# Spreading the gate grids of a PEER layer over 60 blocks, accumulating gathered rows beside them, and holding two gathered rows in flight in the value stage

## The chip, the core and the metric

The kernel runs on one core of a Trainium2 chip. The metric is the device time of one execution in microseconds, the median of several runs; lower is better. In the profile PE is TensorE, PEld its weight loads, DVE is VectorE, ACT is ScalarE, POOL is GpSimd and SP is SyncE; a trailing q marks the queue of an engine that issues DMAs.

## The reference, cut to what matters

One layer of a conditioned hybrid decoder runs on 512 prompt tokens and 64 sample tokens (576 in all). Its first half (norm, input projection, three kinds of mixers, output projection) is not touched. Its second half is PEER: 16384 single-neuron experts, of which each token chooses 16 in each of 8 heads.

```python
q = (xb @ w_q).reshape(PEER_BLOCK, PEER_HEADS, 2, PEER_DQ // 2)
scores = jnp.einsum('bhsd,hskd->bhsk', q, sub_keys).astype(jnp.float32)
sv, si = lax.top_k(scores, PEER_TOPK)
...
top_v, top_pos = lax.top_k(cand, PEER_TOPK)
eidx = jnp.take_along_axis(cidx, top_pos, axis=-1)
gate = jax.nn.softmax(top_v, axis=-1)
u_sel = jnp.take(u_tab, eidx, axis=0)
act = jax.nn.gelu(jnp.einsum('bhkd,bd->bhk', u_sel, xb))
v_sel = jnp.take(v_tab, eidx, axis=0)
return jnp.einsum('bhk,bhkd->bd', gate * act, v_sel)
```

Here `u_tab` and `v_tab` hold 16384 rows of 2048 floats each. So each token's output is a sum of 128 rows of the value table, each weighted by its gate times its activation.

## The kernel before

The tokens are in two groups. For 320 of them, the dense tokens, the kernel multiplies the whole value table with a coefficient matrix (expert by token, zero where an expert was not chosen). For the other 256, the row tokens, it gathers the chosen value rows with indirect DMAs, 128 tokens at a time: gather `s` fetches for each of 128 tokens one row of 2048 floats, and there are 256 gathers (`NSP`), 128 for each half of the row tokens. All matrix products of this half are made of three products each (high times high, low times high, high times low part), so each weight block needs its high part, rounded by ACT (`high`), and its low part, a subtraction on DVE (`low`).

The second half of the program runs in these stages:

- Query blocks, then **row blocks**: 128 blocks of the table `peer_ut`, each times the 256 row tokens. Their activations go to a table in memory. Beside them DVE finds the top 16.
- **Gate stage**: the next 30 blocks of `peer_ut` (a second pass over the table), each times the 320 dense tokens. Beside them the gate grids are made: for each group of 4 dense tokens (80 groups) DVE makes one-hot matrices (L1713 to L1715, three operations, called a hot set here), PE multiplies them (`gate_products`, L2273: four 128x128 products, each of them two instructions in the trace, "x8"), ACT copies the grid out of PSUM into one of two staging tiles (L1065), and after 8 groups ACT sends a staging tile to `gate_scratch`. The loop runs `GL` = 5 times over 6 blocks and 16 grids; PE makes a grid after every sixth of the 96 chunks of such a turn (a block has 16 chunks, a chunk is three products, L2210 to L2212). The double-buffered one-hot tiles lie in the region that begins at `C0`, and so do both staging tiles.
- **Plain stage**: the remaining 98 blocks of `peer_ut`, which end at block `NB_ALL` = 272. Since the staging tiles lie where gathered rows go (`v_rows`, four places), gathers can start only once the last staging tile is saved. DVE adds 120 gathers (`NSP_EARLY`) here, one or two behind a `low`, from the eighth block on (`rows_block`), by a multiply and add of 128x2048 floats each (L1735, `add_rows`).
- **Value stage**: 256 steps (`UNITS`), each a half row block of `peer_v`: ACT rounds it (L1090), DVE subtracts (L1749), PE does 8 chunks of three products (L2299 to L2301). Coefficient factors come back from memory every 8 steps (`load_factors`), are multiplied (L1755), rounded and split (L1759). Every 8 steps DVE adds eight PSUM banks to an accumulator (L1770, `add_half`). The other 136 gathers are added here, at five of every eight steps at most (`rows_step`).

Every engine works through its instructions in program order, and semaphores order the engines. A block or half block lies in a ring (three blocks, six halves): SP loads the next when PE is done with the one before it in the ring. On POOL, `act_column` fetches one column of activations for the row tokens (128 single numbers) and `value_rows` one gather. Before, POOL fetches the first 128 columns during the gate stage, then waits for the saved staging tiles, then issues a column and a gather alternately. Gather `s` waits until DVE has used gather `s-4`, so up to four are under way or waiting in their places.

```python
def value_rows(s):
    if s >= ROWS:
        pool.wait_ge(rows_used, s - ROWS + 1)
```

Of the kernel before, what the change touches and what calls it, by code (L numbers as in the profile page):

```python
# [7 lines left out]
ALU = mybir.AluOpType  # L8
# [7 lines left out]
P = 128  # L16
# [21 lines left out]
NSP, NSP_EARLY = 256, 120  # L38
# [37 lines left out]
def build(nc, a, o):  # L76

    ctx = ExitStack()
    with ctx:
# [179 lines left out]
        stage = [at(C0 + s * NK * TBLK, NK * TBLK).rearrange("p (i t) -> p i t", t=TBLK) for s in range(2)]  # L259
        o_j = [at(C0 + 8192 + s * 512, 512).rearrange("p (t n) -> p t n", n=P) for s in range(2)]  # L260
        o_i = [at(C0 + 9216 + s * 512, 512).rearrange("p (t n) -> p t n", n=P) for s in range(2)]
# [18 lines left out]
        v_rows = [at(C0 + D * k, D) for k in range(ROWS)]  # L280
# [116 lines left out]
        GB = NB_ROWS + 6 * GL  # L397
# [15 lines left out]

        def rows_block(s):
            return GB + 8 + s * (NB_ALL - GB - 8) // NSP_EARLY

# [43 lines left out]
        def _(sp):  # L460
# [108 lines left out]
            for k in range(2):  # L569
                sp.wait_ge(g_saved[k], 16 * (GL + 1))  # L570
            load_value(0)
# [24 lines left out]
        def _(pool):  # L596
# [119 lines left out]
            def act_column(k, s):  # L716
                pool.indirect_dma_start(out=acts[k][:, s:s + 1], out_offset=None, in_=act_table,  # L717
                                        in_offset=bass.IndirectOffsetOnAxis(ap=act_ids[k][:, s:s + 1], axis=0)
                                        ).then_inc(act_in[k], 16)

            def value_rows(s):
                if s >= ROWS:
                    pool.wait_ge(rows_used, s - ROWS + 1)
                pool.indirect_dma_start(out=v_rows[s % ROWS], out_offset=None, in_=v_table,  # L724
                                        in_offset=bass.IndirectOffsetOnAxis(ap=row_ids[s // P][:, s % P:s % P + 1], axis=0)
                                        ).then_inc(rows_in[s % ROWS], 16)
# [4 lines left out]
            for s in range(P):  # L731
                act_column(0, s)
            for k in range(2):
                pool.wait_ge(g_saved[k], 16 * (GL + 1))
            for s in range(NSP):
                if s < P:
                    act_column(1, s)
                value_rows(s)

        @block.scalar  # L740
        def _(act):
# [317 lines left out]
            with act.Fori(0, GL) as w:  # L1059
                for u in range(16):  # L1060
                    k = u // 8
                    if u % 8 == 0:
                        act.wait_ge(g_saved[k], w * 16 + 16)
                    act.wait_ge(g_made, w * 16 + u + 3)
                    act.activation(stage[k][:, :, 4 * (u % 8):4 * (u % 8) + 4].rearrange("p i t -> p t i"),  # L1065
                                   bank(6 + u % 2).rearrange("p (t i) -> p t i", i=P), ACT.Copy).then_inc(g_out, 1)
                    if u % 8 == 7:
                        act.wait_ge(g_out, w * 16 + u + 3)
                        act.dma_start(gd[:, bass.ds(w * 2 + k, 1)].rearrange("p b i t -> p (b i) t"),
                                      stage[k]).then_inc(g_saved[k], 16)  # L1070
                    if u in (1, 4, 7, 9, 12, 15):
                        n = NB_ROWS + (1, 4, 7, 9, 12, 15).index(u)
                        gelu_out(w * 6 + n, n % 3, w * 32 + uses(n), TD)
                        high(None, (n + 2) % 3, w * 32 + 16 * ((n + 2) // 3 + 1))
                        save(w * 6 + n, n % 3, dense_place(w * 6 + n), TD)
# [48 lines left out]
        def _(dve):  # L1124
# [582 lines left out]
            with dve.Fori(0, GL) as w:  # L1707
                step.enter(w, 32)
                for u in range(16):
                    n = w * 16 + u  # L1710
                    dve.wait_ge(g_made, n + 1)
                    idx = [p_selT[:, r, bass.ds(n * 4, 4)].unsqueeze(2).broadcast_to(t4_) for r in range(3)]
                    step(tt(o_e, io, idx[0], ALU.is_equal))  # L1713
                    step(tt(o_i[u % 2], o_e, idx[2], ALU.mult))
                    tt(o_j[u % 2], io, idx[1], ALU.is_equal).then_inc(oh_made, 1)  # L1715
                    if u in (0, 2, 5, 8, 10, 13):
# [683 lines left out]
```

## Time and profile before

| | before |
|---|---|
| median of 3 runs | 4622.29 us (4620.33 to 4625.47) |
| the profiled execution | 4624.3 us, of which the span from first to last instruction is 4622.6 us |
| PE busy | 4352.7 us, 94% of the span |
| DVE busy | 2851.7 us, 62% |
| ACT busy | 1273.7 us, 28% |
| POOL busy | 997.4 us, 22% |
| DMA | 993.88 MB, 215 GB/s in the mean |
| mean granted TensorE clock | 0.957 of full speed |

The shares are means over stages with very different limits. The page also cuts the span into 40 equal slices of about 116 us: there the DMA digit is 4 to 5 in the gate stage and 9 from the plain stage to almost the end, and the clock digit is 8 and 9. What is to be read is the stage from 2572 us, where the dense tokens' blocks begin, to 4576 us, where the value stage's products end.

### The profile page before, as it was taken

To read this page: it belongs to the slowest core of one execution; us is meant where nothing else is said; L and a number is where in the kernel's file an instruction comes from. 1 tells how busy PE (TensorE), PEld (TensorE's weight loads), DVE (VectorE), ACT (ScalarE), POOL (GpSimd) and SP (SyncE) were. 2 spreads that over 40 slices of the span, in tenths; PEclk is the share of its full clock that TensorE was granted. 3 is DMA by queue.
4 is the path that set the end of the run, shared out by engine and by line. 5 is a ranking of instruction groups with operands and counts; after the bars stand their busy time and mean duration, and the time that the engine had idled before them with its cause. 6 is when DMAs were issued, how large, how long until landed. Compare 5 with 4: busy or idle time off the path is not lost.

```text
span 4622.6 us, 71225 instructions
## 1 busy us (share of the span) xinstructions
PE 4352.7 (94%) x29748; PEld 4011.5 (87%) x29748; DVE 2851.7 (62%) x3848; ACT 1273.7 (28%) x1431; POOL 997.4 (22%) x619
## 2 busy tenths in 40 slices
PE   5799999999989699999999888999999999999997
PEld 3577778776679699999999888899999999999997
DVE  0479321323453423888887555477777789888896
ACT  1000101211122212433444344333333333333332
POOL 1000000001100000000000570166666434333440
PEclk8899999998779899999999999999999999999999
DMA  7311212126752222666666444599999999999994
GB/s 302 94 72 41 77 47 79 37 73 233 270 215 99 76 76 84 205 204 204 205 204 205 162 149 149 205 359 368 369 366 374 335 353 362 356 358 350 360 367 157
DMA packets 239177, 993.88 MB, mean 215 GB/s; under 512 B 42920, under 2 KB 117096, under 8 KB 158488
## 3 DMA queue, kind: packets, MB, share of 16 engines
q1 hardware_dynamic: 152376, 652.83, 40.1%
q0 software_dynamic: 48320, 279.88, 15.7%
q10 hardware_dynamic: 38304, 58.74, 3.3%
q8 instruction: 120, 1.97, 0.2%
q14 instruction: 57, 0.47, 0.0%
HBM read 917.71 MB, written 73.64 MB: 214 GB/s over the span
## 4 chain that ended last, share of the span: by engine, by line
PE 83%; DMA 8%; DVE 4%; issue 2%; ACT 2%; DVEq 0%; SPq 0%; ACTq 0%
PE PS L2210 12%; PE PS L2211 12%; PE PS L2212 12%; PE PS L2080 12%; PE PS L2299 5%; PE PS L2300 5%; PE PS L2301 5%; PE PS L2083 5%; DMA arena<-in_peer_v 4%; DMA arena<-in_w_ada 2%; PE PS L1852 2%; PE PS L2189 1%; PE PS L2191 1%; PE PS L2190 1%; PE PS L2273 1%
## 5 line engine op out<-in xcount | busy, mean ns | idle before, releaser
L2210 PE MATMUL PS<-h_hi,blk_hi 128*128 128x256 f32 (+1 forms) x4608 | 1386.4, 301 | 41.0 <-DVE h_lo L1600 32.8
L2211 PE MATMUL PS<-h_lo,blk_hi 128*128 128x256 f32 (+1 forms) x4608 | 1374.8, 298 | 0.0
L2212 PE MATMUL PS<-h_hi,blk_lo 128*128 128x256 f32 (+1 forms) x4608 | 1374.1, 298 | 0.0
L2210 PEld LDWEIGHTS PS<-h_hi,blk_hi 128*128 128x128 f32 x4608 | 885.5, 192 | 44.4 <-issue 22.6
L1606 DVE TENSOR_TENSOR blk_lo<-arena,blk_hi 128x2048 fp32r<-128x2048 f32 x272 | 623.5, 2292 | 454.3 <-ACT blk_hi L998 408.4
L2211 PEld LDWEIGHTS PS<-h_lo,blk_hi 128*128 128x128 f32 x4608 | 885.7, 192 | 0.0
L2212 PEld LDWEIGHTS PS<-h_hi,blk_lo 128*128 128x128 f32 x4608 | 884.4, 192 | 0.0
L724 POOL DMA_INDIRECT arena<-in_peer_v,attw x256 | 561.3, 2193 | 728.2 <-DVE arena L1735 653.9
L2299 PE MATMUL PS<-co_hi,ev_hi 128*128 128x320 f32 x2048 | 636.7, 311 | 23.3 <-DVE ev_lo L1749 17.8
L2300 PE MATMUL PS<-co_lo,ev_hi 128*128 128x320 f32 x2048 | 634.8, 310 | 0.0
L2301 PE MATMUL PS<-co_hi,ev_lo 128*128 128x320 f32 x2048 | 634.5, 310 | 0.0
L2080 PE MATMUL PS<-arena 128*128 128x288 f32 x2176 | 551.4, 414 | 2.2 <-ACT arena L799 2.2
L998 ACT ACTIVATE blk_hi<-arena 128x2048 fp32r<-128x2048 f32 x272 | 518.8, 1907 | 64.0 <-DMA arena<-in_peer_ut 61.4
L2080 PEld LDWEIGHTS PS<-arena 128*128 128x128 f32 x2176 | 417.4, 194 | 120.8 <-issue 2.6
L1090 ACT ACTIVATE ev_hi<-arena 128x1024 fp32r<-128x1024 f32 x256 | 271.7, 1062 | 582.2 <-DMA arena<-in_peer_v 400.3
L2299 PEld LDWEIGHTS PS<-co_hi,ev_hi 128*128 128x128 f32 x2048 | 385.9, 188 | 27.4 <-DVE ev_lo L1749 21.7
L2300 PEld LDWEIGHTS PS<-co_lo,ev_hi 128*128 128x128 f32 x2048 | 386.0, 188 | 0.0
L2301 PEld LDWEIGHTS PS<-co_hi,ev_lo 128*128 128x128 f32 x2048 | 385.9, 188 | 0.0
L717 POOL DMA_INDIRECT attw<-row_activation_scratch,cap x128 | 160.1, 1251 | 1020.2 <-DMA row_activation_scratch<-arena 978.5
L1749 DVE TENSOR_TENSOR ev_lo<-arena,ev_hi 128x1024 fp32r<-128x1024 f32 x256 | 311.4, 1218 | 87.7 <-ACT ev_hi L1090 85.3
L1009 ACT ACTIVATE arena<-PS 128x256 f32<-128x256 f32 (+1 forms) x256 | 105.1, 410 | 871.7 <-PE PS L2212 854.6
L1735 DVE SCALAR_TENSOR_TENSOR arena<-arena,attw 128x2048 f32<-128x2048 f32 x127 | 298.0, 2346 | 3.5 <-DVE arena L1735 0.5
(437 smaller groups left out, 4720.8 us busy)
## 6 DMA issues: line engine op xcount, KB each, us to landing
arena<-in_peer_ut SPq DMA_DIRECT2D x256, 1024.0 KB
arena<-in_peer_v SPq DMA_DIRECT2D x256, 512.0 KB, 8.0
arena<-in_w_ada SPq DMA_DIRECT2D x48, 2048.0 KB, 9.2
arena<-in_w_f SPq DMA_DIRECT2D x17, 2048.0 KB, 8.1
activation_scratch<-arena ACTq DMA_DIRECT2D x128, 160.0 KB
gate_scratch<-arena ACTq DMA_DIRECT2D x10, 2048.0 KB
arena<-activation_scratch SPq DMA_DIRECT2D x32, 640.0 KB, 11.8
arena<-gate_scratch SPq DMA_DIRECT2D x32, 640.0 KB, 14.5
```

The source lines that it names most:

```text
L724: pool.indirect_dma_start(out=v_rows[s % ROWS], out_offset=None, in_=v_table, in_offset=bass.IndirectOffsetOnAxis(ap=row_ids[s // P][:, s ...
L998: act.activation(blk_hi[k][:, :], blk_raw[k], ACT.Copy).then_inc(blk_hi_made, 1)
L1606: tt(blk_lo[k][:, :], blk_raw[k], blk_hi[k][:, :].bitcast(F32), ALU.subtract).then_inc(blk_lo_made, 1)
L1735: ins = stt(acc_rows[k], row, col, acc_rows[k], ALU.mult, ALU.add)
L1749: tt(ev_lo[k % RAWS][:, :], ev_raw[k % RAWS], ev_hi[k % HIS][:, :].bitcast(F32), ALU.subtract).then_inc(ev_lo_made, 1)
L2080: ins = mm(bank(job % 2, 0, HALF), w[:, c, P * (j // 2):P * (j // 2) + P], hT[:, c, HALF * (j % 2):HALF * (j % 2) + HALF], start=c == 0, s ...
L2210: mm(out, hi[:, c], h_part[0][:, c, cols], start=c == 0, stop=False)
L2211: mm(out, hi[:, c], h_part[1][:, c, cols], start=False, stop=False)
L2212: ins = mm(out, lo[:, c], h_part[0][:, c, cols], start=False, stop=c == KC - 1)
L2299: mm(out, ev_hi[k % HIS][:, w], co_hi[n % COS][:, :], start=i == 0, stop=False)
L2300: mm(out, ev_hi[k % HIS][:, w], co_lo[n % COS][:, :], start=False, stop=False)
L2301: ins = mm(out, ev_lo[k % RAWS][:, w], co_hi[n % COS][:, :], start=False, stop=i == RND - 1)
```

## The change

The gate stage now takes 60 blocks (`GBLK` = 12 for each of the 5 turns, still 16 grids a turn), and the plain stage 68. The first staging tile moves out of the gathered rows' region, into the part of the low-part tile of the activations that only the row blocks used, as 16 pieces of 256 columns; the second staging tile and the one-hot tiles are packed into the first three row places. The gathers get a fifth place (`ROWS + 1`), and in the gate stage they use two places, the fourth and the fifth (`row_place`). In the gate stage DVE adds one gather behind each `low` from the fifth block on, 56 in all (`NSP_GATES`); in the plain stage it adds 92 (up to `NSP_EARLY` = 148), with four places as before; 108 are left for the value stage, and from gather 148 on each waits until gather `s-2` is used, so that two are under way. DVE makes each hot set two or more groups ahead of PE. The activation columns come 16 ahead of the gathers (`ACOL`) and are multiplied by their gates in pieces of 16. SP's first value load waits until the 56 gathers are used, since the fifth place lies on its buffer.

```diff
-NSP, NSP_EARLY = 256, 120
+NSP, NSP_GATES, NSP_EARLY = 256, 56, 148
+ACOL, GBLK = 16, 12
...
-        stage = [at(C0 + s * NK * TBLK, NK * TBLK).rearrange("p (i t) -> p i t", t=TBLK) for s in range(2)]
...
+        stage = [at(0, KC * T).rearrange("p (c t) -> p c t", t=T)[:, :, TD:T], at(C0, NK * TBLK)]
...
-        v_rows = [at(C0 + D * k, D) for k in range(ROWS)]
+        v_rows = [at(C0 + D * k, D) for k in range(ROWS + 1)]
...
-        GB = NB_ROWS + 6 * GL
+        GB = NB_ROWS + GBLK * GL
...
+        def row_place(s):
+
+            return (ROWS - 1, ROWS)[s % 2] if s < NSP_GATES else s % ROWS
...
         def rows_block(s):
-            return GB + 8 + s * (NB_ALL - GB - 8) // NSP_EARLY
+            return GB + 3 + (s - NSP_GATES) * (NB_ALL - GB - 4) // (NSP_EARLY - NSP_GATES)
...
+            sp.wait_ge(rows_used, NSP_GATES)
             load_value(0)
...
             def value_rows(s):
-                if s >= ROWS:
-                    pool.wait_ge(rows_used, s - ROWS + 1)
...
+                if row_clear(s):
+                    pool.wait_ge(rows_used, row_clear(s) if s < NSP_EARLY else s - 1)
...
-            for s in range(P):
-                act_column(0, s)
-            for k in range(2):
-                pool.wait_ge(g_saved[k], 16 * (GL + 1))
+            for c in range(ACOL):
+                act_column(c)
+            pool.wait_ge(sel_made, 3)
             for s in range(NSP):
-                if s < P:
-                    act_column(1, s)
+                if s + ACOL < NSP:
+                    act_column(s + ACOL)
+                if s == NSP_GATES:
+                    for k in range(2):
+                        pool.wait_ge(g_saved[k], 16 * (GL + 1))
                 value_rows(s)
...
-                    if u in (1, 4, 7, 9, 12, 15):
...
+                    if u % 4 < 3:
+                        n = NB_ROWS + u // 4 * 3 + u % 4
...
+            one_hots(0)
+            one_hots(1)
+            for b in range(GBLK * GL):
+                low(NB_ROWS + 1 + b, (NB_ROWS + 1 + b) % 3)
+                if b >= GBLK * GL - NSP_GATES:
+                    add_rows(placed)
+                    placed += 1
+                for u in ((2,), (3, 4), (5,))[b % 3]:
+                    if b // 3 * 4 + u < 16 * GL:
+                        one_hots(b // 3 * 4 + u)
...
-                    if at_ % 6 != 5:
+                    if at_ % GBLK != GBLK - 1:
```

DVE at the start of the gate stage, before: the end of the first hot set of a turn, a block's `low` (L1606), and the next hot set (L1713 to L1715). ISA and REGISTER_ALU rows are waits and their arithmetic.

```order
L1715 TENSOR_TENSOR arena<-iota,arena 128x512
L1605 ISA
L1606 TENSOR_TENSOR blk_lo1_60<-arena,blk_hi1_63 128x2048
L1711 REGISTER_ALU
L1713 ISA
L1713 TENSOR_TENSOR arena<-iota,arena 128x512
L66 REGISTER_ALU
L1714 ISA
L1714 TENSOR_TENSOR arena<-arena 128x512
```

DVE in the gate stage, after, from the sixth block's `low` (L1628) on: a gather is added (L1744), then one or two hot sets (L1752 to L1754).

```order
L1628 TENSOR_TENSOR blk_lo0_59<-arena,blk_hi0_62 128x2048
L1744 SCALAR_TENSOR_TENSOR arena<-arena,attw 128x16x128
L1752 TENSOR_TENSOR arena<-iota,arena 128x512
L1753 TENSOR_TENSOR arena<-arena 128x512
L1754 TENSOR_TENSOR arena<-iota,arena 128x512
L1628 TENSOR_TENSOR blk_lo1_60<-arena,blk_hi1_63 128x2048
L1744 SCALAR_TENSOR_TENSOR arena<-arena,attw 128x16x128
L1752 TENSOR_TENSOR arena<-iota,arena 128x512
```

Before, hot sets 0 and 1 of a turn stand on either side of the first `low`; now both are made ahead of the loop, and a gather stands between each `low` and the hot sets behind it.

POOL from the gate stage on, before: 128 columns (L717), then a wait for the saved staging tiles, then columns and gathers (L724).

```order
L717 DMA attw<-row_activation_scratch,cap 128x1 [waits pool_step,a1_saved,a2_saved,a0_saved,idx_made]
L717 DMA attw<-row_activation_scratch,cap 128x1 x127
L717 DMA gla_mask<-row_activation_scratch,siluc 128x1 [waits stage1_saved,stage0_saved]
L724 DMA arena<-in_peer_v,attw 128x2048
L717 DMA gla_mask<-row_activation_scratch,siluc 128x1
```

POOL from the gate stage on, after: the columns are L735 and the gathers L742.

```order
L735 DMA attw<-row_activation_scratch,cap 128x1 [waits pool_step,a1_saved,a2_saved,a0_saved,idx_made]
L735 DMA attw<-row_activation_scratch,cap 128x1 x15
L735 DMA attw<-row_activation_scratch,cap 128x1 [waits sel_made]
L742 DMA arena<-in_peer_v,attw 128x2048
L735 DMA attw<-row_activation_scratch,cap 128x1
```

The first gather moved from behind 129 columns and the staging tiles to behind 17 columns; the wait for the staging tiles now stands in front of gather 56.

## Rows read from the trace of the kernel before

**Rows 1.** Stretches: us, PE, PEld, DVE, ACT, POOL busy; clock; DMA share; GB/s.
```profile
2572.00:2953.00 381.00, 315.39 (x2099) 307.50 (x2098) 227.26 (x269) 153.42 (x141) 160.10 (x128) 0.93 0.42 146
2953.00:3644.00 691.00, 690.09 (x4692) 687.87 (x4691) 496.32 (x219) 224.44 (x196) 439.57 (x249) 1.00 0.96 362
3644.00:4576.00 932.00, 908.66 (x6144) 904.52 (x6144) 807.16 (x811) 319.15 (x384) 337.05 (x135) 0.99 0.92 342
```

**Rows 2.** Timeline of PE, gate stage: start, duration, line, [idle before, releaser].
```profile
2683.05 1.05 PE L2273 MATMUL PS<-arena 128*128 128x128 f32 x8
2686.58 1.05 PE L2273 MATMUL PS<-arena 128*128 128x128 f32 x8
```

**Rows 3.** Timeline of PE, gate stage, around one wait.
```profile
2652.54 0.31 PE L2212 MATMUL PS<-h_hi,blk_lo 128*128 128x320 f32 x1
2655.33 1.86 PE L2273 MATMUL PS<-arena 128*128 128x128 f32 x8 [2.48 <-issue]
```

**Rows 4.** Timeline of ACT and of DVE, gate stage, before the same wait.
```profile
2648.44 0.44 ACT L1009 ACTIVATE arena<-PS 128x320 f32<-128x320 f32 x1 [0.61 <-ACT arena L1065]
2648.78 1.91 ACT L998 ACTIVATE blk_hi<-arena 128x2048 fp32r<-128x2048 f32 x1
...
2650.72 2.29 DVE L1606 TENSOR_TENSOR blk_lo<-arena,blk_hi 128x2048 fp32r<-128x2048 f32 x1 [4.16 <-issue]
2652.92 0.69 DVE L1713 TENSOR_TENSOR arena<-iota,arena 128x512 f32<-128x512 f32 x1
...
2655.20 0.68 DVE L1713 TENSOR_TENSOR arena<-iota,arena 128x512 f32<-128x512 f32 x1
```

**Rows 5.** Who waited for whom in 2572 to 2953: us in total, times, longest.
```profile
PEld PS L2273 <- DVE arena L1715: 43.8, 18, 2.9
...
PEld PS L2273 <- issue: 29.7, 12, 2.9
```

**Rows 6.** Plain stage: one stretch as in rows 1, and DVE's timeline.
```profile
3022.00:3072.00 50.00, 50.00 (x342) 49.80 (x341) 35.54 (x16) 16.52 (x15) 29.45 (x18) 1.00 0.97 379
...
3026.47 4.80 DVE L1735 SCALAR_TENSOR_TENSOR arena<-arena,attw 128x2048 f32<-128x2048 f32 x2
```

**Rows 7.** DMA issues by line: out<-in, count, KB each, median us to landing.
```profile
arena<-in_peer_ut SPq DMA_DIRECT2D x256, 1024.0 KB
...
activation_scratch<-arena ACTq DMA_DIRECT2D x128, 160.0 KB
```

**Rows 8.** POOL's columns: duration ns min/median/max, first and last start.
```profile
L717 POOL DMA_INDIRECT attw<-row_activation_scratch,cap x128: 940/1130/2916, 2579.7 to 2780.3; - x128
```

**Rows 9.** Who waited for whom in 3644 to 4576: us in total, times, longest.
```profile
ACT ev_hi L1090 <- DMA arena<-in_peer_v: 400.3, 151, 15.3
...
PEld PS L2299 <- DVE ev_lo L1749: 21.7, 15, 5.0
```

**Rows 10.** Timeline of DVE, value stage, five gathers in eight steps.
```profile
4200.26 3.57 DVE L1770 TENSOR_TENSOR arena<-arena,PS 128x320 f32<-128x320 f32 x8 [0.99 <-PE PS L2301]
...
4221.89 1.22 DVE L1749 TENSOR_TENSOR ev_lo<-arena,ev_hi 128x1024 fp32r<-128x1024 f32 x1
4223.02 0.48 DVE L1759 TENSOR_TENSOR co_lo<-arena,co_hi 128x320 fp32r<-128x320 f32 x1
4223.43 2.34 DVE L1735 SCALAR_TENSOR_TENSOR arena<-arena,gla_mask 128x2048 f32<-128x2048 f32 x1
4225.69 1.22 DVE L1749 TENSOR_TENSOR ev_lo<-arena,ev_hi 128x1024 fp32r<-128x1024 f32 x1
...
4228.76 3.26 DVE L1770 TENSOR_TENSOR arena<-arena,PS 128x320 f32<-128x320 f32 x8
```

**Rows 11.** Timeline of POOL and DVE, value stage: one gather and its use.
```profile
4414.50 2.41 POOL L724 DMA_INDIRECT arena<-in_peer_v,attw  x1 [11.00 <-issue]
4419.81 1.68 POOL L724 DMA_INDIRECT arena<-in_peer_v,attw  x1 [1.66 <-DVE arena L1735]
...
4424.71 2.35 DVE L1735 SCALAR_TENSOR_TENSOR arena<-arena,gla_mask 128x2048 f32<-128x2048 f32 x1 [0.64 <-DMA arena<-in_peer_v,attw]
```

More of the change, by code:

```diff
@@ L1706, in _ @@
             io = iota[:, :].unsqueeze(1).broadcast_to(t4_)
[L1707 to L1716, printed above, removed]
-                        b = NB_ROWS + 1 + (0, 2, 5, 8, 10, 13).index(u)
-                        low(w * 6 + b, b % 3)
-            step.leave(GL)
             def add_rows(s):
-                if s in (0, P):
-                    k = s // P
-                    dve.wait_ge(act_in[k], 16 * P)
-                    step(tt(acts[k], acts[k], gates[k], ALU.mult))
+                if s == 0:
                     dve.wait_ge(blk_made, NB_ROWS)
+                if s % ACOL == 0:
+                    g, part = s // ACOL, slice(s % P, s % P + ACOL)
+                    dve.wait_ge(act_in[g % 2], 16 * ACOL * (g // 2 + 1))
+                    step(tt(acts[s // P][:, part], acts[s // P][:, part], gates[s // P][:, part], ALU.mult))
                 k, col = s // P, acts[s // P][:, s % P:s % P + 1]
-                row = v_rows[s % ROWS].rearrange("p (c t) -> p c t", t=P)
-                dve.wait_ge(rows_in[s % ROWS], 16 * (s // ROWS + 1))
+                row = v_rows[row_place(s)].rearrange("p (c t) -> p c t", t=P)
+                dve.wait_ge(rows_in[row_sem(s)], row_fills(s))
                 if s in (0, P):
@@ L1738, in _, with one_hots @@
             placed = 0
+            def one_hots(u):
+                dve.wait_ge(g_made, u + 1)
+                idx = [p_selT[:, r, 4 * u:4 * u + 4].unsqueeze(2).broadcast_to(t4_) for r in range(3)]
+                step(tt(o_e, io, idx[0], ALU.is_equal))
+                step(tt(o_i[u % 2], o_e, idx[2], ALU.mult))
+                tt(o_j[u % 2], io, idx[1], ALU.is_equal).then_inc(oh_made, 1)
+            one_hots(0)
[8 more added lines that the diff above has]
+                        one_hots(b // 3 * 4 + u)
+            assert placed == NSP_GATES
             for n in range(GB + 1, NB_ALL):
@@ L2274, in gate_products @@
                     ins.then_inc(g_made, 1)
-                for b in range(6):
-                    block_product(w * 6 + (NB_ROWS + b), (NB_ROWS + b) % 3, (DENSE_COLS,), lambda x: gate_products(x, b))
+                for b in range(GBLK):
+                    block_product(w * GBLK + (NB_ROWS + b), (NB_ROWS + b) % 3, (DENSE_COLS,), lambda x: gate_products(x, b))
             with pe.Fori(0, (NB_ALL - GB) // 3) as i:
```

39 lines of the change are left out of this document (24 added, 15 removed).

## The prediction, made before the changed kernel ran

> **What bounds the kernel now.** I first read the three stretches that the change touches [rows 1]. The gate stage takes 381 us for 30 blocks, with PE busy 315.4 us and its clock at 0.93 in the mean. The plain stage takes 691 us for 98 blocks, PE busy 690.1 us at full clock: 7.05 us a block. The value stage takes 932 us, PE busy 908.7. So in all three PE is the bound where nothing holds it up; the question is what holds it up. In the plain stage nothing does, and DMA stands at 0.96 there with 362 GB/s, while in the gate stage it stands at 0.42 with 146 GB/s. The load on memory is uneven, and so is that on DVE.
>
> Next, PE's timeline in the gate stage. At full pace two grids start 3.53 us apart [rows 2]. Between them lie 18 products of 7.05/48 = 0.147 us, 2.64 us, so a grid costs 0.89 us. The stage's own work is 30 x 7.05 + 80 x 0.89 = 211.5 + 71.2 = 282.7 us. It takes 381, so 98.3 us are lost; 381 - 315.4 = 65.6 of them idle. The list of waits says for whom: a grid waits for DVE's last one-hot 18 times and for "issue" 12 times [rows 5]. The second is the same wait with its releaser not seen: the grid at 2655.33 [rows 3] starts just behind the hot set that ends by 2655.28. That is 30 waits in 30 blocks, one for each. The same grid lasts 1.86 us instead of 1.05 [rows 2, 3]: behind an idle time PE runs at half clock for a while, and that is the other 98.3 - 65.6 = 32.7 us, about 1.1 us a wait.
>
> Why one a block: ACT leaves the block before at 2648.44, rounds the next block's weights from 2648.78 on, DVE, idle for 4.16 us, subtracts from 2650.72 and makes the hot set only behind that, from 2652.92 on, 2.28 us a set [rows 4]. By then PE waits: its products ended at 2652.54 + 0.31 and it needs the set [rows 3]. It is the order of DVE's program, not its load, which is 227 of 381 us [rows 1].
>
> **Term 1, grids over 60 blocks.** Before, the first 60 blocks take 381 + 30 x 7.05 = 592.5 us. After, if no grid waits, they take 60 x 7.05 + 71.2 = 494.2. Gain 98.3. Three blocks and four grids are then 24.7 us. Does DVE fit? Three subtractions at a start-to-start of 2.2 and three gathers at 2.35 make 13.7, four hot sets at 2.28 make 9.1: 22.8 of 24.7 us, 92%. It fits, but barely, so I laid out one turn of three blocks, with 0 at the first block's start, blocks ending at 7.9, 15.9 and 23.8 (grids included), ACT's rounded part ready 2.5 us behind the end of the block before. Block 0: subtraction to about 5.3, gather to 7.65, hot set to 9.95. Block 1: subtraction 10.4 to 12.7, gather to 15.1, hot set to 17.4, and the second hot set must wait for the grid at 18.5 to free its buffer, to 20.8. Block 2: subtraction to 23.1, with the next block starting at 24.7; gather to 25.4, hot set to 27.7, which is 3.0 into the next turn and gives the 5.3 above. So no block waits, with 1.6 us to spare at the tightest place. Each hot set is ready a block before PE asks.
>
> What can still cost here. The gather: gather s is issued when s-2 is used. The uses lie 7.45, 10.3 and 7.0 us apart, so the shortest time from a use to the start of the next but one is 14.4 - 2.35 = 12.1 us. POOL needs 1.7 us to wake, 2.4 to issue, and the one gather on which DVE waited had landed 7.8 us behind POOL's record [rows 11]: 11.9 us, just enough, in a stage with less traffic than that one. The first gather: columns come 1.57 us apart from 2579.7 on [rows 8], so 17 of them end near 2606, the gather lands near 2616, and DVE asks at about 2610; its slack takes most of that. The saves of staging tiles (2 MB at once, 10 times) collide with gathers. I take 6 us for all of this, between 0 and 30 (ten of the 20 turns losing 1.9 us each, and 1.1 of half clock each).
>
> **Term 2, the plain stage gets denser.** A block loads 1.05 MB and saves 0.16 MB [rows 7]; a gather is 128 x 2048 floats, 1.05 MB. Before: 120 gathers over 90 blocks, 1.21 + 1.33 x 1.05 = 2.61 MB in 7.05 us, 370 GB/s. The trace has 362 for the whole stage and 379 for its fullest 50 us, in which PE was never idle [rows 1, 6]. After: 66 block loads 69.2, 68 saves 11.1, 92 gathers 96.5, the last staging tile 2.1, first value loads and factors 2.4: 181.3 MB in 68 x 7.05 = 479.4 us, 378 GB/s. That is the highest rate the trace shows. At 379 it costs nothing, at 375 some 4 us, at 362 the stage takes 501 and it costs 21. DVE has 2.2 + 1.42 x 2.35 = 5.5 of 7.05 us, no bound; two gathers behind one subtraction (4.80 us [rows 6]) and that subtraction just fill a block. I take +5, between 0 and 21.
>
> The Trainium skill (DMA: Bandwidth & Descriptors, "Where 436 GB/s comes from") holds that transfers from memory are bound at about 358 GB/s per core. By that rule the stage would need 506 us and the change would give back 27 us. The trace speaks against it as a ceiling: 379 GB/s over 50 us.
>
> **Term 3, the value stage gets lighter.** Its own work is 256 x 24 x 0.147 = 902 us; it takes 932 with the start, PE idle 23.3. The waits are for DVE's subtraction, behind ACT, which waited 400 us in 151 pieces for value loads [rows 9]. DVE itself is as late: with five gathers, eight steps take it from 4200.26 to 4228.76, 28.5 us, and PE's eight steps are 28.2 [rows 10]. After, 108 gathers instead of 136, 3.6 in eight steps instead of 4.5: 0.9 x 2.27 = 2.0 us less for DVE and 0.94 MB less in 28 us, 33 GB/s. The lost time, 23.3 idle plus some half clock, I put at 25 us, and nearly all of it could go.
>
> What takes some of it back is two in flight. A step with a gather lasts 3.80 us for DVE when it runs freely [rows 10]. Of three gathers in adjoining steps the third is issued when the first is used, 1.7 + 2.1 us of POOL, and lands L later; DVE would want it about 5.3 us behind that use. DVE may be late by some 2 to 3 us before PE notices. Laid out over eight steps, the pattern "three, none, one" loses L - 4.2 us, once in five groups of eight steps (six in all); "three in the middle" loses L - 6.3, also six times; the other three patterns lose nothing until L is about 8. L is at most 7.8 [rows 11], under a full load. At L = 7.8 it is 6 x 3.6 + 6 x 1.5 = 31 us; at 6.5, which I take for the lighter load, 6 x 2.3 + 6 x 0.2 = 15; at 4.2, nothing. I take 12: term 3 is -25 + 12 = -13, between -25 and +6.
>
> The Trainium skill (DMA: Bandwidth & Descriptors, "Anatomy of one DMA") gives 2.0 us plus bytes over 436 GB/s for a DMA from GpSimd, 4.4 us for such a gather. An estimate by that page puts the loss from two in flight at 6 x 0.2, about 1 us, and term 3 at -24. The row with 7.8 us stands against it, at a full load; no run here shows a gather alone.
>
> The columns cost nothing that ends late: POOL is not on any path, and the multiplies in 16 pieces instead of two add perhaps 14 x 0.1 us to DVE. ACT's copies of grids (1.12 us) have a strided target before and after.
>
> **The sum.** -98.3 + 6 + 5 - 13 = -100.3 us. The profiled execution's span is 4622.6 us and its time 4624.3; the span is what the terms are made against, and the median is 4622.3. So 4622.3 - 100.3 = 4522 us, 2.2% faster.
>
> **The rivals.** (a) *The gate stage keeps part of its waits.* DVE is 92% full; if gathers land late or a staging save delays a block, the subtraction slips beyond its 1.6 us and each such slip also costs half clock. At the upper bounds of terms 1 and 2 together it is -98.3 + 30 + 21 - 13 = -60: 4562 us. For it: the 11.9 of 12.1 us. Against it: PE's plain stage ran without a wait at 0.96 DMA. (b) *Two in flight costs nothing and memory keeps up.* Then -98.3 - 25 + 0 to 3: about 4500 us. (c) *Slower: the gathers become the bound.* With two in flight the gathers' latency sets the pace of the value stage. From L = 8 on every pattern loses; at L = 10 the five patterns lose 5.8 + 3.7 + 2.2 + 2.2 + 1.9 a round, 6 rounds, 95 us, and from about L = 10.6, 112 us, it eats all the gains. It would be slower only if a gather took that long with less traffic than now. The one wait of DVE for a gather was 0.64 us [rows 11], yet there were four places. At L = 12 some 155 us are lost: 4665 us. (d) *Memory gives no more in the plain stage than its mean of before.* Then 181.3 MB at 362 GB/s [rows 1] take 501 us, term 2 is +21: 4538 us; against it the 379 of rows 6. By the page of the Trainium skill named in term 2 it would be 4544.
>
> **How the numbers follow.** Forecast (4522, give or take 12) 0.52; (a) 0.20; (b) 0.14; (c) 0.05; (d) 0.05; the rest, 0.04, is a change that doesn't reach its aim for a reason that I don't see and stays within 0.2%. The range leaves out (c), the rest and the outer half of (a): 4498 (all of terms 1 and 3, nothing given back) to 4575. About 0.2% is what a measurement of this kernel can tell from no change. Faster 0.91, same 0.04, slower 0.05.
>
> **What the changed profile would show.** Term 1: 60 blocks in about 500 us at a clock near 1.00, hardly any waits of the grid product for one-hots, DVE at 90% or more; and if (a), waits of a block's first product for the subtraction. Term 2: 68 blocks in about 484 us at 375 GB/s or more, DMA 0.98; if (d), some 501 us at 362. Term 3: DVE waiting for gathers in the value stage, at the third of three in a row, and PE idle about 10 us instead of 23; if (c), idle above 100 us there. The prediction is wrong if DVE's operations get longer beside POOL's, or if hot sets are still made just in time.

## The result, and the profile after

The changed kernel takes 4567.2 us (median of 4 runs, 4559.59 to 4572.01) against 4621.3 us for the kernel before on the same chip (4 runs). The ratio is 0.988, 95% interval 0.9863 to 0.9897: 54 us, 1.2% faster. The forecast was 4522 us, 2.2% faster; the time lies in the range, but the gain is little more than half of what was forecast.

The profiled execution took 4572.0 us, its span is 4570.3. These are its three stretches, with the columns of [rows 1] (us, then PE, PEld, DVE, ACT and POOL busy, clock, DMA share, GB/s): the gate stage, the plain stage and the value stage.

```profile
2580.00:3072.00 492.00, 491.44 (x3507) 491.25 (x3506) 418.19 (x355) 222.55 (x199) 151.32 (x129) 1.00 0.83 305
3072.00:3554.00 482.00, 479.25 (x3259) 477.70 (x3258) 366.18 (x168) 157.74 (x137) 343.87 (x188) 1.00 0.98 381
3554.00:4523.00 969.00, 922.15 (x6147) 916.92 (x6146) 747.60 (x785) 318.69 (x383) 358.52 (x195) 0.98 0.86 300
```

In the first two PE is never idle for more than 0.6%, at full clock. In the third it is idle for 47 us at a granted clock of 0.98; before it was 23.3 us at 0.99 [rows 1]. So the question is the third stretch alone. One view of the first and last starts of a line gives the borders, here of the grid product and of the value stage's first product (duration ns min/median/max, first and last start):

```profile
L2302 PE MATMUL PS<-arena x640: 270/275/275, 2582.7 to 3071.5; 128*128 128x128 f32 x160
its engine sat idle before it (us, times) until:
...
L2328 PE MATMUL PS<-co_hi,ev_hi x2048: 302/309/637, 3554.6 to 4523.1; 128*128 128x320 f32 x187
its engine sat idle before it (us, times) until:
  DVE ev_lo L1778: 98.7, 39
```

Nothing is listed under the grid product: not one of the 80 grids waited, where 30 did [rows 5]. The 98.7 us count both PE's products and its weight loads.

| | before | after | difference | forecast |
|---|---|---|---|---|
| first dense block to first value product | 2572.33 to 3649.35: 1077.0 | 2577.45 to 3554.63: 977.2 | -99.8 | -98.3 + 6 + 5 = -87.3 |
| value stage, first to last chunk | 925.8 | 968.5 | +42.6 | -13 |
| all that is ahead of the dense blocks | 2572.3 | 2577.4 | +5.1 | 0 |

(The dense blocks begin 6 chunks of 0.44 us ahead of the first grid before, 12 after.) The three add up to -52.1 of the -52.3 us between the spans; the last 0.2 lie behind the value stage. The part ahead of the dense blocks has the same program; over the profiled executions of this document its end falls between 2566 and 2577, so that is how executions differ, and I compare stages rather than spans.

What happens in the value stage is seen in one stretch of 25 us, one of the worst. POOL's timeline:

```profile
3778.67 3.49 POOL L742 DMA_INDIRECT arena<-in_peer_v,attw  x1 [10.08 <-DVE arena L1744]
3782.46 5.04 POOL L735 DMA_INDIRECT gla_mask<-row_activation_scratch,siluc  x1 [0.31 <-issue]
3787.80 2.69 POOL L742 DMA_INDIRECT arena<-in_peer_v,attw  x1 [0.30 <-issue]
```

DVE's:

```profile
3781.25 2.34 DVE L1744 SCALAR_TENSOR_TENSOR arena<-arena,gla_mask 128x2048 f32<-128x2048 f32 x1
...
3787.32 2.35 DVE L1744 SCALAR_TENSOR_TENSOR arena<-arena,gla_mask 128x2048 f32<-128x2048 f32 x1 [0.65 <-DMA arena<-in_peer_v,attw]
...
3798.74 2.35 DVE L1744 SCALAR_TENSOR_TENSOR arena<-arena,gla_mask 128x2048 f32<-128x2048 f32 x1 [7.53 <-DMA arena<-in_peer_v,attw]
3801.01 1.22 DVE L1778 TENSOR_TENSOR ev_lo<-arena,ev_hi 128x1024 fp32r<-128x1024 f32 x1
```

And PE's:

```profile
3796.86 0.31 PE L2330 MATMUL PS<-co_hi,ev_lo 128*128 128x320 f32 x1
3802.28 0.64 PE L2328 MATMUL PS<-co_hi,ev_hi 128*128 128x320 f32 x1 [5.11 <-DVE ev_lo L1778]
3802.71 0.47 PE L2329 MATMUL PS<-co_lo,ev_hi 128*128 128x320 f32 x1
3802.98 0.47 PE L2330 MATMUL PS<-co_hi,ev_lo 128*128 128x320 f32 x1
```

DVE is done with one gather at 3783.6, which frees POOL for the next. But POOL is in the middle of a column (until 3787.5), so the gather is issued at 3787.80 and lands 10.9 us later. DVE stands still for 7.53 us with the next subtraction queued behind the gather's addition; PE runs out of subtracted blocks at 3797, waits 5.11 us, and comes back at half clock: products start 0.27 us apart instead of 0.147, and the clock granted from 3802 to 3806 is 0.50. In the waits of the stage DVE stands 139 us for gathers:

```profile
DVE arena L1744 <- DMA arena<-in_peer_v,attw: 139.2, 44, 8.0
PEld PS L2328 <- DVE ev_lo L1778: 52.1, 20, 5.9
PE PS L2328 <- DVE ev_lo L1778: 46.6, 19, 5.6
```

Before, it was 0.64 us once [rows 11]. Pairs of rows of the timelines give how often POOL was late. A gather is freed by the use of the last but one. In 31 of these 44 waits POOL started it 0.3 us behind the end of that addition. In the other 13, which make 45.6 of the 139 us, a column stood in the way, for up to 4.2 us as here. So the column is not in most of the waits; what is in all of them is the time until the gather lands. The profile of after gives that too, as that of before did not. This is the median from the start of POOL's record to the landing, for all gathers:

```profile
arena<-in_peer_v,attw POOLq DMA_INDIRECT x256, 9.4
```

For those of the value stage (asked for L742 from 3554 to 4523; the trace tells the landing of only some of them) it is 9.2:

```profile
DMA to landing us min/median/max: 6.2/9.2/12.9
```

### The profile page after: what moved, and what is told of

It reads as the page before. It is cut to its first block, busy times and chain, and to the rows that moved or that the text cites. A ratio compares the mean times of both kernels' runs of the same rounds, so it can differ in the third digit from the quotient of the medians.

```text
span 4570.3 us, 70640 instructions
## 1 busy us (share of the span) xinstructions
PE 4339.8 (95%) x29748; PEld 4002.6 (88%) x29748; DVE 2856.7 (63%) x3862; ACT 1278.5 (28%) x1431; POOL 914.5 (20%) x619
## 4 chain that ended last, share of the span: by engine, by line
PE 81%; DMA 8%; DVE 8%; POOL 2%; issue 1%; ACT 0%; SPq 0%; DVEq 0%; ACTq 0%; POOLq 0%
PE PS L2239 13%; PE PS L2240 13%; PE PS L2241 13%; PE PS L2109 12%; PE PS L2112 5%; DMA arena<-in_peer_v,attw 4%; PE PS L2328 3%; PE PS L2330 3%; PE PS L2329 3%; PE PS L1881 2%; DMA arena<-in_w_ada 2%; DVE arena L1744 2%; PE PS L2218 2%; PE PS L2220 2%; PE PS L2219 2%; PE PS L2302 1%
## 5 line engine op out<-in xcount | busy, mean ns | idle before, releaser
L2239 PEld LDWEIGHTS PS<-h_hi,blk_hi 128*128 128x128 f32 x4608 | 876.3, 190 | 47.1 <-issue 22.4
L1628 DVE TENSOR_TENSOR blk_lo<-arena,blk_hi 128x2048 fp32r<-128x2048 f32 x272 | 623.2, 2291 | 265.9 <-ACT blk_hi L1018 264.4
L742 POOL DMA_INDIRECT arena<-in_peer_v,attw x256 | 439.9, 1718 | 941.6 <-DVE arena L1744 869.0
L2328 PEld LDWEIGHTS PS<-co_hi,ev_hi 128*128 128x128 f32 x2048 | 390.8, 191 | 52.1 <-DVE ev_lo L1778 52.1
L1744 DVE SCALAR_TENSOR_TENSOR arena<-arena,gla_mask 128x2048 f32<-128x2048 f32 x127 | 298.3, 2349 | 143.9 <-DMA arena<-in_peer_v,attw 140.6
L735 POOL DMA_INDIRECT attw<-row_activation_scratch,cap x128 | 182.5, 1426 | 1016.5 <-DMA row_activation_scratch<-arena 977.8
```

Source lines behind the costliest of these rows:

```text
L742: pool.indirect_dma_start(out=v_rows[row_place(s)], out_offset=None, in_=v_table, in_offset=bass.IndirectOffsetOnAxis(ap=row_ids[s // P][: ...
L1628: tt(blk_lo[k][:, :], blk_raw[k], blk_hi[k][:, :].bitcast(F32), ALU.subtract).then_inc(blk_lo_made, 1)
L1744: ins = stt(acc_rows[k], row, col, acc_rows[k], ALU.mult, ALU.add)
L2239: mm(out, hi[:, c], h_part[0][:, c, cols], start=c == 0, stop=False)
L2328: mm(out, ev_hi[k % HIS][:, w], co_hi[n % COS][:, :], start=i == 0, stop=False)
```

## The experiments

"Value stage" below is the time from the first to the last start of its first product line, 925.8 us before and 968.5 after. Theory A: two gathers in flight are too few for where the gathers stand. Theory B: the memory queues are the limit, and the depth only shows it.

**Four in flight again.** The wait of the changed kernel goes back to "its place is free".

```diff
-                    pool.wait_ge(rows_used, row_clear(s) if s < NSP_EARLY else s - 1)
+                    pool.wait_ge(rows_used, row_clear(s))
```

> The changed kernel with one edit: in the value stage too a gather waits only until its own place is free, so four are under way again; 108 gathers there as in the changed kernel. Theory A (two in flight is what costs): the 139 us in which DVE waited for gathers in the value stage go to under 20, the stage falls from 968 us to 905 to 925, and the time to 4505 to 4525. Theory B (the memory queues are the limit, and two in flight only makes it visible): value loads now land late as before the change, ACT waits for them 350 us or more, the stage stays above 950 us and the time above 4550.

Measured: 4505.8 us (4500.2 to 4517.1), ratio to the kernel before on the same chip 0.9739 (0.9714 to 0.9764). The value stage takes 912.7 us. The waits of the same stage:

```profile
ACT ev_hi L1112 <- DMA arena<-in_peer_v: 308.2, 114, 14.8
...
PEld PS L2328 <- DVE ev_lo L1778: 7.7, 7, 4.5
PE PS L2328 <- DVE ev_lo L1778: 5.8, 5, 4.3
```

Theory A: no wait of DVE for a gather is listed in the stage, and it takes 56 us less. What theory B said of ACT is partly there (308 us of waits for value loads, up to 14.8 at a time, against 230 in the changed kernel), but PE hardly notices. With fewer gathers in flight the value loads landed sooner (6.2 us in the median against 7.0), and that was worth nothing.

**Three in flight.**

```diff
-                    pool.wait_ge(rows_used, row_clear(s) if s < NSP_EARLY else s - 1)
+                    pool.wait_ge(rows_used, row_clear(s) if s < NSP_EARLY else s - 2)
```

> The changed kernel with three gathers in flight in the value stage instead of two. Theory A: the third of three adjoining gathers is issued one step with a gather (3.8 us) earlier, which covers most of the 3 to 5 us that PE waited at a time; the stage comes to 910 to 922 us and the time to 4503 to 4520, near the run with four. If the loss were from POOL's columns rather than the depth, three would stay above 4540.

Measured: 4505.9 us (4502.3 to 4508.7), ratio 0.9726 (0.9703 to 0.9749), value stage 916.3 us. The third gather in flight is worth nearly all of it; between three and four lie 4 us of the stage in one execution of each, and nothing in the medians.

**No gathers in the value stage.** The last 108 gathers, their additions and the last 96 columns are left out.

```diff
-NSP, NSP_GATES, NSP_EARLY = 256, 56, 148
+NSP, NSP_GATES, NSP_EARLY = 148, 56, 148
...
-                if s + ACOL < NSP:
+                if s + ACOL < 160:
```

> The changed kernel without the last 108 gathers, their additions and the last 96 columns: the 108 largest parts of the row tokens' sums are left out, the rest is computed. This is the floor of the value stage. Both theories expect PE without a wait there: 256 x 24 x 0.147 = 902 us and a few us at its start, 903 to 912 us; more than 920 would mean that something other than gathers holds the stage.

Measured: 4506.4 us in one run, value stage 907.8 us. That is the floor, and the two runs above stand at it: with three or four in flight 108 gathers of 1 MB cost some 5 to 9 us in their stage.

**Two in flight in the kernel before.**

```diff
-                    pool.wait_ge(rows_used, s - ROWS + 1)
+                    pool.wait_ge(rows_used, s - ROWS + 1 if s < NSP_EARLY else s - 1)
```

> The kernel before with one edit: from gather 120 on, so in the value stage alone, a gather waits until the last but one is used (two under way instead of four); 136 gathers there. Theory A (a gather needs about 9 us from POOL's record to landing, so two in flight starve DVE): the value stage grows from 926 us by 60 to 130 us and the time to 4680 to 4750. Theory B (memory queues are the limit, fewer in flight relieve the value loads): the stage gets no longer, the time stays within 15 us of before.

Measured: 4745.6 us (4741.4 to 4750.9), ratio 1.025 (1.0225 to 1.0274), value stage 1054.4 us: this one edit costs 129 us there. With 136 gathers in place of 108 the same depth costs more than twice as much. So the change was made of a part that gains and a part that loses, and the gain of moving 28 gathers away hid how large the loss is.

```profile
L2299 PE MATMUL PS<-co_hi,ev_hi x2048: 302/309/637, 3637.5 to 4691.9; 128*128 128x320 f32 x187
...
  DVE ev_lo L1749: 209.2, 100
```

**All columns before the value stage.** Two in flight stay; the plain stage fetches two columns ahead of each gather, the value stage none. The columns from the seventh group of 16 on count on other semaphores (`LATER`), since more of them are under way.

```diff
-                if s + ACOL < NSP:
-                    act_column(s + ACOL)
+                if s < NSP_GATES:
+                    act_column(s + ACOL)
+                elif s < NSP_EARLY:
+                    for c in range(2):
+                        act_column(NSP_GATES + ACOL + 2 * (s - NSP_GATES) + c)
```

> The changed kernel with two in flight kept, but all activation columns are fetched before the value stage (two columns ahead of each gather of the plain stage instead of one), so that POOL has only gathers to issue there. Theory A1 (half of the lateness is the column that POOL issues between two gathers, 3.5 to 5 us): the value stage falls by 25 to 45 us and DVE's wait for gathers there from 139 to about 60 us. Theory A2 (it is the gather's own transfer): under 10 us gained. In both the plain stage may lose a few us to POOL.

Measured: 4628.8 us (4616.7 to 4643.3), ratio 1.0005 (0.9989 to 1.0021). The value stage falls to 942.9 us, 26 less, the low end of what A1 said. But DVE's wait for gathers there falls only to 115 us, not 60, and the plain stage, where I expected a few us, loses 88 (570.7 us instead of 483.0): the value stage begins at 3636. POOL's timeline in the plain stage shows why:

```profile
3209.78 1.90 POOL L739 DMA_INDIRECT attw<-row_activation_scratch,cap  x1 [0.30 <-issue]
3211.98 0.94 POOL L739 DMA_INDIRECT attw<-row_activation_scratch,cap  x1 [0.30 <-issue]
3213.23 0.95 POOL L751 DMA_INDIRECT arena<-in_peer_v,attw  x1 [0.30 <-issue]
3214.48 2.90 POOL L739 DMA_INDIRECT attw<-row_activation_scratch,cap  x1 [0.30 <-issue]
3217.69 1.90 POOL L739 DMA_INDIRECT attw<-row_activation_scratch,cap  x1 [0.31 <-issue]
3219.89 0.94 POOL L751 DMA_INDIRECT arena<-in_peer_v,attw  x1 [0.30 <-issue]
```

It issues without a pause, and a gather comes every 6.7 us, while the stage uses one every 7.05/1.42 = 5.0 us. A column of 128 single numbers takes POOL at least as long as a gather of 1 MB (1.9 us in the median against 0.95 in this stage). In the plain stage POOL had been the next bound all along (343.87 of 482 us in its records, and 0.3 us between each two), and I had looked only at where it waited.

**Half gathers.** The 108 gathers of the value stage fetch 1024 floats a row, from other places of the table, so the row tokens' sums are others.

```diff
-                pool.indirect_dma_start(out=v_rows[row_place(s)], out_offset=None, in_=v_table,
+                half = s >= NSP_EARLY
+                pool.indirect_dma_start(out=v_rows[row_place(s)][:, 0:D // 2] if half else v_rows[row_place(s)],
+                                        out_offset=None, in_=v_halves if half else v_table,
```

> The changed kernel, but the 108 gathers of the value stage fetch 1024 floats a row instead of 2048 (0.5 MB), from other places of the table, so the row tokens' sums are not the reference's; DVE adds as many floats as before. Two in flight. If a gather's time is mostly its bytes, it lands some 3 us sooner and the value stage falls from 968 to 910 to 930 us; if it is mostly fixed (POOL's issue and completion), it stays above 945.

Measured: 4557.2 us in one run, value stage 951.7 us. Half the bytes bring back 17 of some 56 us. It is tempting to conclude that a gather's time is mostly fixed: of the gathers on which DVE waited, the time from the start of POOL's record to their use has a median of 9.1 us in the changed kernel (44 of them, 5.4 to 14.5) and of 7.9 us here (35 of them, 5.0 to 12.2). But these are the late ones alone, picked by their lateness. Over all gathers of the stage of which the trace tells the landing, it is 6.4 us instead of the 9.2 above:

```profile
DMA to landing us min/median/max: 4.1/6.4/12.2
```

So the gathers did land some 3 us sooner, as the first half of the expectation has it, and the stage did not fall to 910 to 930 all the same. What is left is the column: again 13 waits stand behind one, and here they make 58.7 of DVE's 102 us.

**Both of these.** Half gathers, and all columns before the value stage.

> The changed kernel, two in flight, with both edits: all columns before the value stage, and the 108 gathers of the value stage at half their bytes (so the row tokens' sums are not the reference's). Alone they took the value stage from 968 to 943 and to 952 us. If the gather's lateness is a sum of column, bytes and a fixed rest, the stage comes to 918 to 932; if it reaches the floor of 908 to 912, no fixed rest holds it.

Measured: 4592.9 us in one run, of which the plain stage has again some 80 us more; the value stage takes 916.6 us, between the two ranges that were expected. Alone the edits gave 26 and 17 us, together 52: somewhat more than their sum, and within 9 us of the floor. So what costs is the whole of POOL's column, POOL's issue and the transfer against one fixed window; no part is the cause by itself.

**At most two adjoining steps.** The gathers stand at steps 2, 3, 5 and 6 of every eight.

```diff
-            places = [k for k in range(6, UNITS - 12) if 2 <= k % RND <= 6]
+            places = [k for k in range(6, UNITS - 12) if k % RND in (2, 3, 5, 6)]
```

> The changed kernel with two in flight, and the value stage's gathers placed at steps 2, 3, 5 and 6 of every eight instead of 2 to 6, so that no three stand at adjoining steps. Theory A as predicted (only runs of three lose): the loss of 57 us against the stage's floor halves or better, time 4525 to 4545. If a gather is late by more than one step, the third still lands late, at step 5, and the time stays at 4555 or above.

Measured: 4573.9 us (4568.8 to 4577.4), ratio 0.9874 (0.985 to 0.9898), value stage 979.4 us against 968.5. Nothing is gained; whether something is lost is not shown, since the ratio agrees with that of the changed kernel (0.988). My reading of the loss, three in a row with the third a little late, was wrong. From a use at step 2 to the addition at step 5 there are 10.6 - 2.35 = 8.2 us, and POOL's start (0.3) and 9.2 to landing make 9.5; a column in the way adds up to 4.2. DVE waited 39 times here, 128.4 us; 15 of the waits stand behind a column, and they make 81.6 of it.

**Every other step.** Two in flight, gathers at the odd steps only.

```diff
-            places = [k for k in range(6, UNITS - 12) if 2 <= k % RND <= 6]
+            places = [k for k in range(6, UNITS - 12) if k % 2]
```

> The changed kernel with two in flight, and the value stage's gathers placed at the odd steps only (119 places for 108 gathers), so that from the use of one to the use of the next but one there are four steps, 14.1 us, mostly. Theory A with the sizes measured meanwhile (1.7 us for POOL to wake, 9 us from the start of its record to landing, up to 14, a column of 1 to 5 us between): the window of 14.1 - 2.35 = 11.7 us covers the middle gather; PE's loss against the floor falls from 60 us to 10 to 30, the time to 4515 to 4540. If two in flight were too few at this average rate whatever the order, it stays above 4555.

Measured: 4512.3 us (4510.4 to 4518.6), ratio 0.9757 (0.9729 to 0.9786), value stage 914.7 us. It is 3 us below the range that was expected. DVE still waits for gathers:

```profile
DVE arena L1744 <- DMA arena<-in_peer_v,attw: 73.1, 26, 5.2
...
PEld PS L2328 <- DVE ev_lo L1778: 10.5, 11, 5.0
```

but each time for less, up to 5.2 us instead of 8.0, and PE has enough subtracted blocks in hand. No wait stands behind a column: POOL starts every gather on which DVE waits 0.3 us behind the addition that frees it (the 1.7 us in the expectation is a misreading, see below). Two in flight are enough for 108 gathers in 238 steps if no window from a use to the next but one is shorter than four steps.

The steps follow from `rows_step`, the waits from the timelines. The table sorts the gathers of the value stage by their window, from the end of one use to the start of the next but one. It gives on how many gathers DVE waited, of how many, and how long in all:

| window | changed kernel | pairs | every other step | two in the kernel before |
|---|---|---|---|---|
| two steps, 4.7 us | 15 of 15, 49.3 us | | | 63 of 67, 167.6 us |
| three steps, 8.2 us | 29 of 33, 89.9 us | 37 of 43, 121.8 us | | 8 of 9, 24.7 us |
| four steps, 11.8 us | | 2 of 5, 6.6 us | 26 of 86, 73.1 us | |
| five or more, 15.3 us | 0 of 58 | 0 of 58 | 0 of 20 | 0 of 58 |

**The order of DVE's program alone.** In the kernel before, with 30 blocks in the gate stage, only the place of the subtraction among the hot sets is moved.

```diff
-                    if u in (0, 2, 5, 8, 10, 13):
-                        b = NB_ROWS + 1 + (0, 2, 5, 8, 10, 13).index(u)
+                    if u in (1, 4, 7, 9, 12, 15):
+                        b = NB_ROWS + 1 + (1, 4, 7, 9, 12, 15).index(u)
```

> The kernel before with one edit: in the gate stage of 30 blocks DVE's subtraction for the next block stands behind hot sets 1, 4, 7, 9, 12 and 15 of a turn instead of 0, 2, 5, 8, 10 and 13. Grids, blocks and gathers are as before. Theory O (the lost 98 us came from the order of DVE's program, not from how many grids a block has): the waits of grids for one-hots nearly go, the stage falls from 381 us to 285 to 320, the time to 4525 to 4565. Theory S (the grids have to be spread over more blocks): under 20 us gained, above 4600.

Measured: 4532.0 us (4531.0 to 4540.3), ratio 0.9799 (0.9779 to 0.9818). The stretches of its gate, plain and value stage:

```profile
2567.00:2853.00 286.00, 286.00 (x2114) 286.00 (x2113) 230.73 (x271) 154.01 (x140) 185.87 (x128) 1.00 0.56 197
2853.00:3545.00 692.00, 690.48 (x4693) 687.76 (x4692) 496.35 (x219) 225.88 (x197) 445.17 (x249) 1.00 0.95 361
3545.00:4475.00 930.00, 906.37 (x6111) 903.02 (x6110) 803.00 (x800) 318.51 (x384) 330.98 (x135) 0.99 0.92 343
```

and the grid product, under which no wait is listed:

```profile
L2273 PE MATMUL PS<-arena x640: 269/275/276, 2574.0 to 2853.4; 128*128 128x128 f32 x160
its engine sat idle before it (us, times) until:
who waited for it (us, times):
  ACT arena L1065: 116.6, 61
```

From 2571.3 to 2853.5 the 30 blocks and 80 grids take 282.1 us; the stage's own work was worked out as 282.7. Six numbers in DVE's program give the whole of term 1, and this kernel is 35 us faster than the changed one. What spreading the grids brings on top is room for gathers beside them: with four in flight the changed kernel is another 26 us faster (4506 against 4532). Between the two profiled executions it is 24; of those the value stage gives 17 (929.8 against 912.7 us), the dense blocks give 2 (981.2 against 979.0), and 5 lie ahead of them, where the programs are the same.

## Why the prediction was right, and where it was off

**What bounds the kernel** held: PE at 0.147 us a product everywhere, and waits of two kinds on top. The reading of the gate stage (order, not load; 65.6 us idle and 32.7 of half clock) was borne out to less than a microsecond by the run with the order alone. That the 12 waits put down to "issue" were waits for the same one-hot is seen in the run with two in flight in the kernel before, whose gate stage has the same program. There all 30 waits of PE for the grid product, and all 30 of its weight loads, are named (2567 to 2950):

```profile
PEld PS L2273 <- DVE arena L1715: 73.8, 30, 2.9
PE PS L2273 <- DVE arena L1715: 65.9, 30, 2.6
```

**Term 1** (-98.3, +6 held back): 60 blocks took from 2577.4 to 3071.6, 494.2 us, as worked out. DVE does its work in the order of the hand-laid turn; it is busy for 85% of the stage (418.19 of 492 us), where 90% or more was foretold. The +6 was not needed. The first gather was late, by 4.97 us of DVE's time, and no grid felt it.

**Term 2** (+5): the plain stage took 483.0 us against 479.4, at 381 GB/s in the mean:

```profile
3113.00:3163.00 50.00, 49.99 (x340) 49.55 (x339) 38.84 (x19) 16.49 (x14) 34.08 (x19) 1.00 1.01 395
3163.00:3213.00 50.00, 50.00 (x343) 50.00 (x342) 39.73 (x19) 16.46 (x14) 40.65 (x22) 1.00 1.00 389
```

Memory gave 395 GB/s over 50 us, more than the highest rate seen before (379 in [rows 6]), which had been demand and no ceiling. Rival (d) is out, and with it the bound at about 358 GB/s per core of the Trainium skill (DMA: Bandwidth & Descriptors, "Where 436 GB/s comes from") for this single core.

**Term 3** (-13, measured +42.6) is where it was off, above all in one term of its sum, the +12 for two in flight. Without it the stage gains 13 us (the run with four in flight: 912.7 against 925.8), half of the 25 that I put down; 6 of the 25 are not the gathers' at all, since the stage takes 907.8 us without any, against 902 worked out. With two in flight it loses 56. What was wrong in the working of the +12:

- *Which gathers are late.* It priced three gathers at adjoining steps and held that "the other three patterns lose nothing until L is about 8". But all windows of two steps and nearly all of three lose (the table above). The first products of each eight steps say where PE lost time, against 28.2 us a round: in the 11 rounds with steps 2, 3, 4, 6 or 3, 4, 5, the two patterns that were priced, 9.6 us; in the other 18 rounds 50.3 us, of them 34.0 in the nine with steps 2, 3, 5, 6. So the term was put at nothing where most of the loss lies. Behind the first round PE lost time only in every other one, in which POOL's records of the waited gathers are longer (3.5 us in the median against 1.7); why is not shown.
- *POOL's column.* "The columns cost nothing that ends late" rested on POOL waiting most of the time. But POOL issues the next column directly behind a gather, and where the next gather is freed meanwhile, it waits for up to 4.2 us. In all 13 cases it is the gather of step 6, eight of them with steps 2, 3, 5, 6. Of PE's 59.9 us, 44.6 fall in the 13 rounds in which a waited gather stood behind a column. The early columns brought 26 us back.
- *The sizes.* "POOL needs 1.7 us to wake" is a misreading: the 1.66 in [rows 11] is how long POOL had been idle. The addition that released it is the row of DVE shown below: it ended at 4419.54, and POOL started at 4419.81, 0.27 us behind. "L is at most 7.8" came from the one row in which DVE had waited; a single wait is a sample, and the trace of before could not show the slower gathers, since four places hid them. From the end of POOL's record the waited gathers of after took 7.2 us in the median, 15 of 44 more than 7.8, up to 10.5. In the median these two errors cancel, and more: 1.7 + 2.1 + 7.8 = 11.6 us were reckoned from a use to the landing, and 0.3 + 9.2 = 9.5 measured. So latency alone, put into the forecast's own table, would not have given the loss (it comes to about 9 us there); the windows and the columns do.

```profile
4417.16 2.38 DVE L1735 SCALAR_TENSOR_TENSOR arena<-arena,gla_mask 128x2048 f32<-128x2048 f32 x1
```

That the time lies in the range is in part luck. The upper end of 4575 had been set for waits in the gate stage, which did not come; term 3 ran 37 us over its own bound of +6. With the other terms as forecast the sum would have been 4578; the +6 that term 1 did not need brought it inside. The forecast of "faster" rests on term 1, and that was understood.

**The rivals.** (c), the gathers' latency as the bound of the value stage, comes nearest to what happened, in a chance of 0.05. But it asked for L = 10 in the median to lose 95 us, and the runs show 56 at 7.2; and it had its price as all or nothing ("slower"), while the mechanism acts in part. The forecast's upper end of +6 for term 3 should have left room for it. (a) did not come true in any part. (b), near 4500 us, is what the changed kernel is with one more gather in flight. The Trainium skill's figure for a DMA from GpSimd (DMA: Bandwidth & Descriptors, "Anatomy of one DMA"), 2.0 us plus bytes over 436 GB/s, gives an estimate of 4.4 us for a gather and about 1 us of loss; the median to landing in the value stage is 9.2 us, beside 300 GB/s of traffic in the mean, and the loss 56. The measurement decides against it in this place.

The best kernel of these runs is the changed one with three or four gathers in flight, 4506 us, 2.6 to 2.7% faster than before and 1.3% faster than the change as it was made.

## What to carry to other kernels

A depth of transfers in flight is to be set by the shortest window between uses, not by the mean rate: count from the use that frees the place through the issuing engine's start, whatever else it issues first, and the landing, and compare it with the time until the engine asks. When an engine waits for a small piece of work that another makes in program order, look first at the order in which that engine makes its pieces; here six numbers gave 98 us that a new layout of the stage also gave. A rate or a latency read from a trace in which nothing waited is no bound; it is what was asked for. The number in the brackets of a row is the idle time of the engine, not its delay behind the releaser. And when two edits are compared by a latency, it is to be taken over all transfers and not over those that were waited for.

## What the runs showed of the hardware

- One core reads and writes at 381 GB/s over 480 us and at 395 GB/s over 50 us, with block loads, gathers and stores together.
- An indirect DMA of 128 single numbers costs POOL about as much as one of 128 rows of 8 KB. Both take 0.94 us at the least. In the changed kernel's value stage the medians are 1.2 us for a column (up to 5.1) and 1.7 us for a gather (up to 5.0); with two columns for each gather in the plain stage they are 1.9 and 0.95. What makes some of them long was not tried.
- POOL starts 0.3 us behind the addition that frees it, when it is idle (the median of 127 such starts in the value stage of before, 78 after).
- A gather of 1 MB in the value stage of after lands 9.2 us behind the start of POOL's record in the median (6.2 to 12.9), and 6.4 us with half the bytes (4.1 to 12.2).
- PE's products start 0.27 us apart behind a wait of 5.11 us, at a granted clock of 0.50, as behind one of 2.48 us before, and 0.147 us apart at full clock.
